# Routing tables of a mixture-of-experts block: marks made by one VectorE instruction per pick, last table products earlier, first gathers from the index table itself

## The reference

```python
hn = rms_norm(h, norm2_g[l]).reshape(bsz * s, d)
eidx, gates = route(hn, w_router[l], router_bias[l])          # top 8 of 64 experts for each token
routed = routed_experts(hn, eidx, gates, w_gate[l], w_up[l], w_down[l])
shared = (jax.nn.silu(hn @ ws_gate[l]) * (hn @ ws_up[l])) @ ws_down[l]
h = h + (routed + shared).reshape(bsz, s, d)
...
return rms_norm(h, final_norm_g)

def routed_experts(...):      # assignments sorted by expert, padded to blocks of 128 rows
    def step(y, blk):
        tok, gate, e = blk
        xb = x_pad[tok]
        h = jax.nn.silu(xb @ w_gate[e]) * (xb @ w_up[e])
        out = (h @ w_down[e]) * gate[:, None]
        return y.at[tok].add(out), None
```

## Time and profile before

| | us |
|---|---|
| median of 3 runs | 1331.91 (1330.11 to 1332.43) |
| profiled execution, whole time | 1332.42 |
| its span in the trace | 1330.7 |
| PE busy | 1279.6 (96%) |
| DVE busy | 863.9 (65%) |
| ACT busy | 802.6 (60%) |
| POOL busy | 461.8 (35%) |
| mean DMA rate | 254 GB/s |

### The profile page before, as it was taken

How to read it: one execution, slowest core, us unless ns; L and a number is a source line. 1 busy time by engine, 2 the same in 40 slices (tenths; PEclk the granted TensorE clock), 3 DMA queues, 4 the chain that set the end, 5 groups by cost and what they waited for, 6 DMA issues and landing times.

```text
span 1330.7 us, 26943 instructions
## 1 busy us (share of the span) xinstructions
PE 1279.6 (96%) x6095; PEld 1039.1 (78%) x6096; DVE 863.9 (65%) x1228; ACT 802.6 (60%) x1083; POOL 461.8 (35%) x604
## 2 busy tenths in 40 slices
PE   6999999999867999999999999999999999999996
PEld 5885467888646888888888888888888888888885
DVE  6430464558633677777776777767776777767767
ACT  5320254233586667677766767677776777677763
POOL 2432301000002443434444444444443344444464
PEclk9999999999988999999999999999999999999999
DMA  9204033211407899999999999999999999999989
GB/s 339 97 1 158 0 133 120 95 64 72 159 32 248 271 302 357 302 329 314 340 322 337 319 316 348 312 339 322 352 317 333 318 347 334 308 321 324 347 238 266
DMA packets 81268, 337.65 MB, mean 254 GB/s; under 512 B 12624, under 2 KB 15696, under 8 KB 64592
## 3 DMA queue, kind: packets, MB, share of 16 engines
q1 hardware_dynamic: 53872, 251.19, 48.9%
q0 software_dynamic: 27360, 86.01, 26.6%
HBM read 288.59 MB, written 65.27 MB: 266 GB/s over the span
## 4 chain that ended last, share of the span: by engine, by line
PE 87%; DVE 4%; issue 3%; ACT 3%; DMA 2%; POOL 1%; POOLq 0%; ACTq 0%; SPq 0%; DVEq 0%
PE ps L847 38%; PE ps_out L861 19%; PE ps L507 7%; PE ps L524 7%; PE ps L657 6%; PE ps L560 4%; PE ps L708 2%; PE ps L869 1%; ACT mark L1151 1%; DMA yb_in<-y_rows_dram 1%; PE ps_out L690 1%; PE ps L608 1%; DVE pick L1653 1%; DVE ya_in L1769 1%; DMA g_row<-in_norm_g 0%
## 5 line engine op out<-in xcount | busy, mean ns | idle before, releaser
L847 PE MATMUL ps<-w_gu,xTh 128*128 x1488 | 468.7, 396 | 2.3 <-DVE xTl L1692 2.3
L1489 DVE TENSOR_TENSOR w_gu<-raw_gu,w_gu (+1 forms) x256 | 296.7, 1221 | 76.0 <-ACT w_gu L1158 73.0
L847 PEld LDWEIGHTS ps<-w_gu,xTh 128*128 128x128 f32 x1488 | 274.0, 188 | 55.6 <-issue 2.9
L847 PE MATMUL ps<-w_gu,xTl 128*128 x744 | 291.7, 392 | 0.0
L1158 ACT ACTIVATE w_gu<-raw_gu (+1 forms) x256 | 250.2, 1051 | 0.8 <-issue 0.8
L861 PE MATMUL ps_out<-w_dn,hTh 128*128 x744 | 242.2, 407 | 0.0
L1904 POOL DMA_INDIRECT y_rows_dram<-ob,idxs x90 | 146.6, 1628 | 150.7 <-ACT ob L1181 143.6
L1496 DVE TENSOR_TENSOR w_dn<-raw_dn,w_dn (+1 forms) x128 | 151.4, 1224 | 27.6 <-ACT w_dn L1162 23.1
L847 PEld LDWEIGHTS ps<-w_gu,xTl 128*128 128x128 f32 x744 | 140.1, 188 | 28.9
L861 PEld LDWEIGHTS ps_out<-w_dn,hTh 128*128 128x128 f32 x744 | 133.1, 189 | 25.4 <-issue 0.2
L861 PE MATMUL ps_out<-w_dn,hTl 128*128 x372 | 145.9, 392 | 0.0
(11 more groups left out here) (291 smaller groups left out, 1704.3 us busy)
## 6 DMA issues: line engine op xcount, KB each, us to landing
raw_gu<-in_w_gate SPq DMA_DIRECT2D x64, 1024.0 KB, 6.8
raw_gu<-in_w_up SPq DMA_DIRECT2D x64, 1024.0 KB, 10.8
raw_dn<-in_w_down SPq DMA_DIRECT2D x64, 1024.0 KB, 12.8
x_ring<-in_x SPq DMA_DIRECT2D x8, 512.0 KB, 4.8
w_in_sb<-in_w_in SPq DMA_DIRECT2D x8, 512.0 KB, 9.9
xh<-in_x SPq DMA_DIRECT2D x8, 512.0 KB, 8.0
w_out_sb<-in_w_out SPq DMA_DIRECT2D x1, 4096.0 KB, 12.9
hn_rows_dram<-rows SPq DMA_DIRECT2D x8, 512.0 KB, 2.6
```

The lines of the kernel that those rows point to most:

```text
L847: mm = pe.matmul(ps[3][:, :], x_[:, k, :], w_gu[:, bass.ds(at, 1), part, :, k, :], start=(k == 0 and part == 0 and x_ is xTh), stop=(k == ...
L1489: dv.tensor_tensor(gu_part(w_gu[:, :, 1, :, :, :], at, m), gu_part(raw_gu, at, m), gu_part(w_gu[:, :, 0, :, :, :], at, m).bitcast(F32), AL ...
```

## The change

- `count8` and `new_mark` are gone, with GpSimd's fill of the first and the wait for it. The semaphore `s_mtok` is gone.
- A second cast (`item8f`, float32) is made of the items beside `item8`.
- `two_marks` makes 16 `tensor_scalar` instructions (2 chunks, 8 picks), each over 136 columns of `count_row`: equal to the item of the pick, times the token, both read as one value per partition. They write `mark` directly. It waits for them, then makes `pick` as before and raises `s_pick`, for which `table` now waits.
- `marks_by_token` is gone from ACT, and `high_x(6)` and `high_x(7)` stand earlier in its queue.
- `shared_h(5)` stands ahead of `rest_x(6)` and `two_marks(2)` on DVE.
- `two_tables(3)` stands ahead of `shared_turn(6)` on TensorE.
- The first three gathers read their indices from `idx_all` itself, without the copy to `idxg`; the later ones do as before.

```diff
@@ -139,8 +139,7 @@
         gb_row = place("gb_row", [P, DA], F32, R_AT + 10 * KB)
         pick = [place("pick0", [P, 2, TOPK, P], F16, R_AT), place("pick1", [P, 2, TOPK, P], F16, R_AT + 6 * KB + 256)]
         rt_a = place("rt_a", [P, NC, NE], F32, R_AT + 4 * KB)
-        count8 = place("count8", [P, TAB, TOPK], F16, W_AT)
-        new_mark = place("new_mark", [P, 2, TAB, TOPK], F16, W_AT + 2176)
+        item8f = place("item8f", [P, NC, TOPK], F32, W_AT)
         hs2 = place("hs2", [P, 2, F], F32, W_AT + 10624)
         hh2 = place("hh2", [P, 2, F], F32, W_AT + 10624 + 2 * KB)
         Xg_first = place("Xg_first", [P, GATED], F32, W_AT + 16 * KB)
@@ -272,7 +271,6 @@
         s_htq, s_hqh, s_hql = (sem(n) for n in ("shared_h_tr", "shared_hT_high", "shared_hT_rest"))
         s_yst = [sem("h_stored_low"), sem("h_stored_mid"), sem("h_stored_high")]
         s_shst = [sem("shared_stored0"), sem("shared_stored1")]
-        s_mtok = sem("marks_times_token")
         s_mask, s_chunks, s_cols = sem("mask_ready"), sem("chunks_ready"), sem("item_cols_ready")
         s_kinds = sem("kinds_ready")
         s_rv, s_pm, s_tab = sem("routing_step"), sem("routing_matmul"), sem("tables_ready")
@@ -738,7 +736,7 @@
                 mm.then_inc(s_sdn, 1)
 
             def table(c):
-                pe.wait_ge(s_mtok, c // 2 + 1)
+                pe.wait_ge(s_pick, c // 2 + 1)
                 for k in range(TOPK):
                     mm = pe.matmul(ps[5][:, 0:TAB], pick[c // 2 % 2][:, c % 2, k, :], mark[:, c % 4, k, :],
                                    start=(c == 0 and k == 0), stop=(c == NC - 1 and k == TOPK - 1))
@@ -822,9 +820,9 @@
             shared_down(3)
             two_tables(2)
             shared_gu(7, (0, 1))
+            two_tables(3)
             shared_turn(6)
             shared_gu(7, (2, 3))
-            two_tables(3)
             shared_down(4)
             shared_turn(7)
             shared_down(5)
@@ -1141,17 +1139,6 @@
                     act.activation(ob[:, 1, 0:512], ps[0][:, :], ACT.Copy)
                     act.activation(ob[:, 1, 512:D], ps[4][:, :], ACT.Copy).then_inc(s_y0, 1)
 
-            def marks_by_token(pair):
-                act.wait_ge(s_pick, pair + 1)
-                if pair >= 2:
-                    act.wait_ge(s_table, 2 * (pair - 1))
-                at = pair % 2 * 2
-                for r in range(2):
-                    c = 2 * pair + r
-                    ins = act.activation(mark[:, at + r, :, :].rearrange("p k j -> p j k"), new_mark[:, r, :, :], ACT.Copy,
-                                         scale=token[:, c:c + 1])
-                ins.then_inc(s_mtok, 1)
-
             def split_gu(at, parts):
 
                 for m in parts:
@@ -1239,19 +1226,15 @@
             high_x(5)
             shared_high_h(3)
             shared_silu(4)
-            marks_by_token(0)
+            high_x(6)
             shared_out(1)
-            high_x(6)
             shared_high_h(4)
             shared_silu(5)
-            marks_by_token(1)
+            high_x(7)
             shared_out(2)
-            high_x(7)
-            marks_by_token(2)
             shared_high_h(5)
             shared_silu(6)
             shared_out(3)
-            marks_by_token(3)
             act.wait_ge(s_rg, 1)
             act.wait_ge(s_cl, SPLITS + NC - 2 + NC)
             split_gu(1, (0, 1))
@@ -1632,36 +1615,32 @@
             step(dv.tensor_tensor(rt_b[:, :, :], rt_b[:, :, :], mask[:, :, :], ALU.mult))
             many(dv.max(slot8[:, c, :], rt_b[:, c, :]) for c in range(NC))
             step(dv.tensor_scalar(item_i[:, :, :], slot8[:, :, :], 1.0 / P, 0.5 + 0.5 / P, ALU.mult, ALU.subtract))
-            step(dv.tensor_copy(item8[:, :, :], item_i[:, :, :]))
+            many((dv.tensor_copy(item8[:, :, :], item_i[:, :, :]), dv.tensor_copy(item8f[:, :, :], item_i[:, :, :])))
             step(dv.scalar_tensor_tensor(out=place8[:, :, :], in0=item8[:, :, :], scalar=-float(P), in1=slot8[:, :, :],
                                          op0=ALU.mult, op1=ALU.add))
             dv.wait_ge(s_pm, 4)
             dv.tensor_copy(tab[0:3, 0:P], ps[5][0:3, 344:344 + P]).then_inc(s_tab, 1)
             rest_x(5)
             shared_rest_h(3)
-            dv.wait_ge(s_info, 4)
-
             def two_marks(pair):
 
-                if pair >= 1:
-                    dv.wait_ge(s_mtok, pair)
                 if pair >= 2:
                     dv.wait_ge(s_table, 2 * (pair - 1))
                 both = slice(2 * pair, 2 * pair + 2)
-                many((dv.tensor_tensor(new_mark[:, :, :, :], count8[:, None, :, :].to_broadcast([P, 2, TAB, TOPK]),
-                                       item8[:, both, None, :].to_broadcast([P, 2, TAB, TOPK]), ALU.is_equal),
-                      dv.tensor_tensor(pick[pair % 2][:, :, :, :],
+                many(dv.tensor_scalar(mark[:, c % 4, k, :], count_row[:, 0:TAB], item8f[:, c, k:k + 1], token[:, c:c + 1],
+                                      ALU.is_equal, ALU.mult) for c in range(2 * pair, 2 * pair + 2) for k in range(TOPK))
+                many((dv.tensor_tensor(pick[pair % 2][:, :, :, :],
                                        count_row[:, None, None, 1:P + 1].to_broadcast([P, 2, TOPK, P]),
-                                       place8[:, both, :, None].to_broadcast([P, 2, TOPK, P]), ALU.is_equal)))
+                                       place8[:, both, :, None].to_broadcast([P, 2, TOPK, P]), ALU.is_equal),))
                 dv.sem_inc(s_pick, 1)
 
             two_marks(0)
             shared_h(4)
             two_marks(1)
             shared_rest_h(4)
+            shared_h(5)
             rest_x(6)
             two_marks(2)
-            shared_h(5)
             shared_rest_h(5)
             rest_x(7)
             two_marks(3)
@@ -1861,21 +1840,21 @@
 
             for c in range(NC):
                 rstd(3, c, s_sq2, s_r2)
-            gp.wait_ge(s_wo, NC)
-            gp.iota(count8[:, :, :], pattern=[[1, TAB], [0, TOPK]], base=0, channel_multiplier=0,
-                    allow_small_or_imprecise_dtypes=True).then_inc(s_info, 1)
-
-
             top_row = gp.to_reg(S - 1)
             top_dump = gp.to_reg(2 * ROWS - 1)
 
             def gather(i, u):
 
-                gp.tensor_copy(idxg[:, u:u + 1], idx_all[:, bass.ds(i, 1)]).then_inc(s_gi, 1)
-                gp.wait_ge(s_gi, i + 1)
+                if isinstance(i, int) and i < TURN:
+                    column = idx_all[:, i:i + 1]
+                    gp.sem_inc(s_gi, 1)
+                else:
+                    column = idxg[:, u:u + 1]
+                    gp.tensor_copy(column, idx_all[:, bass.ds(i, 1)]).then_inc(s_gi, 1)
+                    gp.wait_ge(s_gi, i + 1)
                 gp.sem_inc(s_turn, 1)
                 gp.indirect_dma_start(out=Xg_first[:, :] if isinstance(i, int) and i == 0 else Xg[:, u, :], out_offset=None, in_=hn_d[:, :],
-                                      in_offset=bass.IndirectOffsetOnAxis(ap=idxg[:, u:u + 1], axis=0),
+                                      in_offset=bass.IndirectOffsetOnAxis(ap=column, axis=0),
                                       bounds_check=top_row, oob_is_err=False).then_inc(s_ga[u], 16)
 
             def keep_gate(i, u):
```

## The result

| | before | after |
|---|---|---|
| median of 4 executions, us | 1332.12 | 1311.90 (1311.83 to 1312.15) |
| ratio, 95% interval | | 0.9852 [0.9835, 0.9869] |
| span of the profiled execution, us | 1330.7 | 1310.4 |
| TensorE busy, us (share) | 1279.6 (96%) | 1275.0 (97%) |
| ACT mark instructions | 8, 5.2 us each | none |

The change saves 20.2 us, where 25.8 were forecast. The whole gain, and somewhat more, is there before `shared_down(4)` ends. Seven microseconds of it are lost again in the next 37.

The account below looks back on a forecast made before the run. TensorE, 96% busy, was taken as the bound, waiting on ACT's marks during the index table. A gain of 27.1 us at `shared_down(4)` less 1.3 for the collision gave -25.8, from 1331.9 to 1306 us; range 1301 to 1314.

Parts of the forecast that it names:

- The instruction: Each new DVE mark `tensor_scalar`: 306 ns if both halvings apply, at a pitch of 0.23 us, 6.3 us a pair.
- The second rival: DVE marks don't reach the fast rate: pitch 0.33 us, 6.4 us more, 1312.5 us; chance 0.15.
- the first: Pointer reads on DVE are hidden, pitch below 0.17 us, TensorE paces the stretch: 1302 to 1303.5 us; chance 0.15.
- The schedule: Index table beside the shared expert: `shared_down(4)` ends at 385.0 instead of 412.1, a gain of 27.1 us.
- waits of 0.7, 1.3 and 0.6 us: TensorE waits for DVE ahead of `shared_turn(4)` (0.7), `shared_gu(6)` (1.3) and the moved `two_tables(3)` (0.6).
- The clock: TensorE's granted clock stays at 1.0 from 353 to 395 us.
- The hand-over: From `shared_down(4)` to the first `gate_up`: down-weight loads collide with chunk 4's store, costing 0 to 3 us, taken as 1.3.
- the first sign: Gain found at `shared_down(4)` (385) but not at the first `gate_up` (forecast at 396): the store is to blame.
- The moves: Reordered queues: table products 3 and ACT's `high_x` gain nothing; `shared_h(5)` earlier on DVE spares TensorE waiting for pair 2.
- Gathers without copies: First gathers on GpSimd: 0.2 to 2.2 us saved there, none of it counted in the total.
- The third: The load and store collision takes more, or the 1.3 us wait drops the clock: 1309 to 1314 us; chance 0.12.

Follow-up runs that it names:

- the kernel with copies: The changed kernel with the copies of index columns put back in the first three gathers: 1309.8 us, ratio 0.9842 to the kernel before.
- the two buffers: The changed kernel with buffers of their own for the shared results of chunks 6 and 7: 1304.73 us, ratio 0.9797 to the kernel before.
- the kernel before with one edit: The kernel before with `new_mark` laid out pick outside, item inside, so ACT reads and writes marks in the same order: 1310.68 us.
- late loads and better order: The two buffers, plus first down-weight loads behind the stores of chunks 4 and 5, and DVE marks and `two_tables(3)` reordered: 1304.54 us.

## Why the prediction was right in the sum and wrong in a step

The time, 1311.9, lies in the range (1301 to 1314) and 5.9 us above the forecast of 1306.

- **The instruction.** Foreseen 306 ns and a pitch of 0.23, from one element with an immediate, one pointer and f32 rows; measured 305 ns and 0.226. By the prediction's sum that is both halvings, for f16 and for a single source. The second rival (0.33) and the first (below 0.17) fall. The Trainium skill ("Vector Engine (DVE) Microarchitecture Reference", section 5.2) has about 75 ns after overlap. The prediction's estimate from it, 110 ns, is under half of the measured pitch; it has no term for the two pointers.
- **The schedule.** Foreseen waits of 0.7, 1.3 and 0.6 us, measured 0.49, 1.08 and, ahead of table products 3, 0.14 (377.83 to 377.97). The first was 0.2 too long by a slip in the sum: 358.68 less 2.73 and 0.15 is 355.8, not 355.6. `shared_down(4)` was to end at 385.0 and ended at 384.8: a gain of 27.3 for 27.1. That DVE paces it was shown by making the marks twice.
- **The clock.** Foreseen 1.0 from 353 to 395, measured 1.00 from 353 to 396 and then 0.72 and 0.50. The forecast took the first `gate_up` at the full clock. It ran in 8.02 us and not 5.73: 2.3 of the missing 5.9 us.
- **The hand-over, the term that was mis-sized.** "That costs between 0 and 3 us; I take 1.3": it cost 5.0. The prediction named the store, its place behind the loads, and the first sign by which it would be found (385 right, first `gate_up` late). The size was wrong since it charged the loads alone and only a part of them. It had the store 3.9 us behind the loads, and of these it says "5 to 6 us of the queue"; no row shows that figure, they landed 7.4 us after their issue in the kernel before and 10.9 in the change. The store came 3.05 us behind them, when 0.07 MB had moved, so all but 0.1 of their 2.1 MB still stood ahead of it. The gathers had no price at all, and while the store was under way they took 24.4% of the engines' time, 2.6 of 10.59 us. Two gathers taken out made the store 2.7 us shorter, its place ahead of the loads 4.5. The hand-over is 3.7 us above its term; with the clock's 2.3, less 0.2 of gain above the forecast at `shared_down(4)`, that makes 5.8 of the 5.9 us.
- **The moves.** Table products 3 were taken at nothing. They brought the gathers 2.9 us ahead, into the time of the loads and the store: undone, the time is 4.8 us less in the median (in three executions of four) and the wait of 5.64 us is gone, though the run doesn't part the gathers from the longer distance between loads and store.
- **Gathers without copies.** Taken at nothing, as found.
- **The rivals.** The third (more for the collision, 1309 to 1314, chance 0.12) happened. It gave the clock's drop to the wait of 1.3 us in the shared expert; the trace has it behind the wait for the store instead. That the range held is in part luck: the hand-over lies outside its 0 to 3 us, and the prices that the prediction had for this course, 3 us for the store and 1.9 for the clock, come to 1309.7. The end of 1314 rests as much on rival 2, a slower DVE, which didn't happen.

What the prediction never asked is why ACT took 5.2 us for 1088 elements. The Trainium skill ("ScalarE: Activation LUTs", section "What ACT_TABLE_LOAD costs") has 186 ns, 0.833 ns for an element and 93 ns for a pointer: 1185 ns as an estimate, under a quarter of the 5.23 us. The measured 1195 ns agree with it once the write is in order. With that question the same gain would have been had for one index pattern.

**Open.** What lowers the clock for a `gate_up` isn't settled. `gate_up(1)` comes behind a wait of 1.72 us in the change (7.36 us) and in the kernel with copies (5.76 us), each behind a longer wait of 5.64 or 5.92 and a slow `gate_up(0)`. Behind nearly the same wait it takes 7.36 us with the two buffers (1.72) and 5.74 in the kernel before with one edit (1.75), each time with a `gate_up(0)` at the full clock ahead. Nor was the two-buffer kernel run with the table products in their old place.

## What to carry to other kernels

Ask of an instruction on the chain what its elements should cost before you move it to another engine: here its access order was the price, and mending that alone gave the whole gain. When a stage moves forward by 27 us, list every transfer that now falls within 10 us of another, in all queues, with bytes over the measured rate, and follow which buffer's reuse waits for each. A buffer of its own, which removes the wait, was worth 5.7 us and a better place in the queue 4.3 (their executions overlap), and the two together less than either (1.7).

## What the runs showed of the hardware

- An ACT write of 2-byte elements, 272 bytes apart, runs at 4.8 ns an element (5.23 us for 1088), and the same in order at 1.1 ns (1.20 us). Function, pointer scale and count were equal, and both read their elements one after the other.
- A DVE `tensor_scalar` of 136 f16 elements with two pointer scalars takes 305 ns and follows the one ahead every 0.226 us. Compares of 2176 f16 elements with a second input spread along the innermost dimension take 2.42 us, 1.11 ns each, so the 16 small instructions (3.7 us, multiplication included) do the work of one such compare and two ACT instructions (4.8 us). The Trainium skill ("VectorE: DVE Perf Modes", section "The TRN2 errata") advises tiles of 512 elements or more. The rows agree for DVE, which is busy for 3.7 us with the small form and for 2.4 with the large one; in the whole time the two aren't told apart (1311.9 and 1311.0).
- A store of 0.5 MB took 5.1 us in the kernel before, about 6.1 ahead of two loads of 1 MB, 7.9 behind them, and 10.6 behind them with two more gathers beside it.
- The granted clock stayed at 1.00 over three waits of at most 1.1 us in 40 us, and was at 0.50 after one of 5.64 us: a `gate_up` of 5.5 us at the full clock then took 8.0. It also stayed at 1.00 from 384 to 424 over four waits of 0.52 to 1.30 us (late loads and better order). Behind waits of 1.71 to 1.75 us it fell in some kernels and stayed in others.
